# Attention over pairs of heads: transposes of scaled probabilities, one instruction per pair, queues shifted by a pair

## The chip, the cores and the metric

One core of one Trainium2 chip. The time is that of one execution of the program on the device, in microseconds (us). Engines: TensorE (PE; its weight loads are listed as PEld), VectorE (DVE), ScalarE (ACT), GpSimd (POOL) and SyncE (SP, which issues the DMAs). L1972 is line 1972 of the kernel before; in the kernel after, the same code stands up to 8 lines earlier, and the transposes are recorded at the helper `turn` (L1572 there).

## The reference, cut to what matters

A two-layer backbone over 256 context and 256 latent tokens of width 1024 in float32. Each layer has a gated FFN, a mixer and a second gated FFN. The mixer of the second layer is neighbourhood attention: 16 heads of 64, latent queries on a grid of 4 rows by 64 columns, softmax over the local window and all context keys together.

```python
s_loc = jnp.where(col_valid[:, :, None, :], s_loc + bias, NEG_INF)
s_ctx = jnp.einsum('bjqhd,bkhd->bhjqk', qb, k_c).astype(jnp.float32)
s = jnp.concatenate([s_loc.reshape(B, H, n_cb, NA_QBLOCK_W, n_loc), s_ctx], axis=-1)
p = jax.nn.softmax(s, axis=-1).astype(v_g.dtype)
...
o = (jnp.einsum('bhjqil,bijlhd->bjqhd', p_loc, v_blk)
     + jnp.einsum('bhjqk,bkhd->bjqhd', p_ctx, v_c))
```

## The kernel before

The program is written by hand: each engine has one list of instructions, and semaphores tie them together. The large projections run as three passes each of values split into a high and a low part (`three`, L1582 to L1586). ScalarE makes the high parts, VectorE the low ones, SyncE fetches weight tiles two ahead.

Both mixers have a function `mixer1` or `mixer0` on every engine. The attention is the last part of `mixer1`, after the keys, queries and values are projected. It has 32 units, one for each head and half of the 256 queries. Two heads that lie in the two 64-partition halves of one tile make a pair with the same half of the queries, so there are 16 pairs; `pair_of(j)` gives the tile (j // 2), the half s, and `at`, the first of the pair's two places among four (0 or 2). Everything is sized 128 queries by 512 keys per unit. For unit u of pair j:

- TensorE `scores_of` (L1960): one fp32 matmul with 64 rows, the two heads side by side in the two halves of the array, into one PSUM bank each. Pairs take turns between `ps_all[0:2]` and banks 2 and 3. From pair 2 on it waits for the exponentials of pair j - 2.
- VectorE `maxima`: adds the bias to the 256 local keys in PSUM (L1464), takes the negated maximum over 512 keys (L1467). One instruction per unit.
- ScalarE `exps` (L889): exponential from PSUM to SBUF, and the row's sum through the accumulator. The results lie in `prob`, which uses the buffers named scaled and normed.
- VectorE `diagonals`: the reciprocal of the sum (L1476), then the identity times it, a diagonal of 128x128 (L1480).
- TensorE `turn_probs` (L1972): four matmuls of a 128x128 block of the probabilities against the diagonal, which turn and normalise it in one step, into `ps[1]`, one bank per unit. `ps[1]` has no second copy, so the turn waits for the copy of the pair before.
- ScalarE `copy_turned` (L899): from PSUM to `prob_t`, 512 elements per unit.
- TensorE `outputs_of` (L1985): eight matmuls with 64 output rows, two heads side by side, for the pair before.
- every second pair, ScalarE `high` (L904) and VectorE `low` (L1486) split a finished tile for the projection na_out.

The order of each queue is set by these loops: TensorE `turn_probs(j)`, `scores_of(j + 2)`, `outputs_of(j - 1)`; ScalarE `copy_turned(j)`, `exps(j + 2)`; VectorE `maxima(j + 2)`, `diagonals(j + 2)`. After the last outputs, TensorE goes on with na_out, whose last step waits for the last split.

`turn` (L1578) is a helper used elsewhere in the program: `pe.transpose` against the identity. Lines 1729 (fp32 matmuls of 128x128), 962 (an operation of 1024 elements), 1086 and 1384 (VectorE in the norms and in the first mixer), 1308 and 1309 (VectorE, 512 elements) and 877 (a ScalarE copy of 1024 elements from PSUM) belong to other stages and serve the prediction as prices.

## Time and profile before

| | |
|---|---|
| median of 3 runs | 1903.8 us (1902.56 to 1903.91) |
| profiled execution | 1899.26 us, span 1897.5 us, mean granted clock 0.976 |
| PE busy | 1813.9 us (96% of the span) |
| DVE busy | 1207.3 us (64%) |
| ACT busy | 748.8 us (39%) |
| attention, first scores to last outputs | 1588.6 to 1656.9 us from the span's start |

The span runs from the first to the last instruction of the profiled execution; its own time lies 1.8 us above. Busy times are shares of the whole span and mix stages with different limits. Times of rows are microseconds from the span's start. A fp32 matmul is two records on PE, a transpose one. Where two matmuls run side by side in two halves of the array, each has its own records.

### The profile page before, as it was taken

How to read it: one execution, taken by the hardware profiler on the slowest of the kernel's cores; microseconds unless marked ns; L12 is line 12 of the kernel's file. 1: busy time of each engine (PE TensorE's matmuls, PEld its weight loads, DVE VectorE, ACT ScalarE, POOL GpSimd, SP SyncE). 2: the span in 40 equal slices, each digit the busy share in tenths (PEclk: the TensorE clock that was granted, in tenths of full speed). 3: DMA queues.
4: the chain of work that ended last, by engine and by line, in shares of the span. 5: the costliest groups of instructions: out<-in, count | busy, mean ns of one | idle time of the engine just before them, and what ended most of it. 6: DMA issues, size and time to landing. Idle time of an engine off the chain costs nothing.

```text
span 1897.5 us, 25311 instructions
## 1 busy us (share of the span) xinstructions
PE 1813.9 (96%) x9680; PEld 1531.0 (81%) x9680; DVE 1207.3 (64%) x1908; ACT 748.8 (39%) x1067; POOL 62.7 (3%) x40
## 2 busy tenths in 40 slices
PE   6899999999989798999999999999999999989998
PEld 2788888877788587888888878888887797789998
DVE  4777677778999744876677367766333435655554
ACT  2522122347888734222222352222223434654343
POOL 0000000020000010000000200000002000010001
PEclk8999999999999998999999999999999999989999
DMA  7454555331110122544553344453323341034553
GB/s 300 156 188 163 181 190 209 113 115 67 47 55 34 45 89 101 190 185 150 196 210 117 114 155 177 150 190 147 111 69 108 122 167 45 1 127 169 178 183 120
DMA packets 39860, 257.74 MB, mean 136 GB/s; under 512 B 4688, under 2 KB 5840, under 8 KB 14832
## 3 DMA queue, kind: packets, MB, share of 16 engines
q1 hardware_dynamic: 39792, 256.86, 37.3%
q8 instruction: 40, 0.66, 0.1%
q14 instruction: 28, 0.23, 0.0%
HBM read 255.79 MB, written 1.05 MB: 135 GB/s over the span
## 4 chain that ended last, share of the span: by engine, by line
PE 84%; DVE 9%; ACT 4%; issue 2%; DMA 1%; SPq 0%; DVEq 0%; ACTq 0%
PE ps_all L1582 26%; PE ps_all L1586 26%; PE ps_all L1583 25%; DVE w_lo L950 2%; PE ps_all L1972 2%; PE bank L1630 1%; DMA start_scale<-in_w_scale 1%; ACT w_hi L535 1%; PE bank L1985 1%; DVE sq_acc L1300 1%; PE bank L2008 1%; PE ps_all L1960 0%; DVE normed L1309 0%; DVE wb L1264 0%; DVE scaled L1291 0%
## 5 line engine op out<-in xcount | busy, mean ns | idle before, releaser
L1582 PE MATMUL ps_all<-a_hi,w_lo 128*128 128x512 f32 (+1 forms) x1800 | 663.2, 368 | 21.4 <-ACT a_hi L645 14.2
L1586 PE MATMUL ps_all<-a_lo,w_hi 128*128 128x512 f32 (+1 forms) x1800 | 657.9, 366 | 0.2 <-DVE a_lo L1089 0.2
L1583 PE MATMUL ps_all<-a_hi,w_hi 128*128 128x512 f32 (+1 forms) x1800 | 657.4, 365 | 0.0
L950 DVE TENSOR_TENSOR w_lo<-w_raw,w_hi 128x2048 fp32r<-128x2048 f32 (+3 forms) x184 | 376.5, 2046 | 162.7 <-ACT w_hi L535 161.6
L535 ACT ACTIVATE w_hi<-w_raw 128x2048 fp32r<-128x2048 f32 (+3 forms) x183 | 313.5, 1713 | 332.0 <-PE ps_all L1586 324.1
L1582 PEld LDWEIGHTS ps_all<-a_hi,w_lo 128*128 128x128 f32 x1800 | 345.4, 192 | 79.4 <-issue 16.5
L1586 PEld LDWEIGHTS ps_all<-a_lo,w_hi 128*128 128x128 f32 x1800 | 345.1, 192 | 56.6 <-DVE a_lo L1089 4.1
L1583 PEld LDWEIGHTS ps_all<-a_hi,w_hi 128*128 128x128 f32 x1800 | 345.8, 192 | 51.8 <-issue 0.2
L962 DVE SCALAR_TENSOR_TENSOR mod_junk<-mod_raw,cond 128x1024 bf16<-128x1024 f32 x256 | 302.7, 1220 | 5.0 <-ACT cond L563 2.7
L1582 PE MATMUL ps_all<-g_hi,w_lo 128*128 128x512 f32 (+1 forms) x704 | 257.8, 366 | 1.2 <-DVE w_lo L950 1.2
L1586 PE MATMUL ps_all<-g_lo,w_hi 128*128 128x512 f32 (+1 forms) x704 | 256.3, 364 | 0.0
L1583 PE MATMUL ps_all<-g_hi,w_hi 128*128 128x512 f32 (+1 forms) x704 | 254.3, 361 | 0.0
L546 ACT ACTIVATE sil<-ps_all 128x512 f32<-128x512 f32 (+1 forms) x88 | 47.8, 543 | 483.6 <-PE ps_all L1586 483.5
L988 DVE TENSOR_TENSOR gated<-sil,ps_all 128x512 f32<-128x512 f32 (+1 forms) x88 | 54.6, 621 | 193.8 <-ACT sil L546 193.8
L1027 DVE SCALAR_TENSOR_TENSOR h<-ps_all,gate,h 128x256 f32 (+1 forms) x136 | 59.9, 480 | 168.8 <-PE ps_all L1586 168.1
L1586 PEld LDWEIGHTS ps_all<-g_lo,w_hi 128*128 128x128 f32 x704 | 132.2, 188 | 23.2
L1583 PEld LDWEIGHTS ps_all<-g_hi,w_hi 128*128 128x128 f32 x704 | 132.2, 188 | 22.0
L1582 PEld LDWEIGHTS ps_all<-g_hi,w_lo 128*128 128x128 f32 x704 | 132.5, 188 | 21.6 <-DVE w_lo L950 1.9
L549 ACT ACTIVATE g_hi<-gated 128x512 f32 (+3 forms) x88 | 51.0, 579 | 69.2 <-DVE gated L988 69.2
L995 DVE TENSOR_TENSOR g_lo<-gated,g_hi 128x512 f32 (+3 forms) x88 | 54.8, 623 | 27.7 <-ACT g_hi L549 27.7
L1547 POOL TENSOR_TENSOR sq_acc<-sq 128x512 f32<-128x512 f32 (+1 forms) x6 | 11.9, 1977 | 1732.0 <-ACT sq L582 1732.0
L645 ACT ACTIVATE a_hi<-scaled,modv,gain 128x256 fp32r<-128x256 f32 x88 | 48.4, 592 | 22.4 <-DVE scaled L1077 22.4
(234 smaller groups left out, 1493.3 us busy)
## 6 DMA issues: line engine op xcount, KB each, us to landing
w_raw<-in_tiles SPq DMA_DIRECT2D x118, 1024.0 KB, 4.7
mod_raw<-in_w_mod SPq DMA_DIRECT2D x64, 1024.0 KB, 4.8
w_raw<-in_tiles SPq DMA_DIRECT2D x32, 768.0 KB, 4.1
w_raw<-in_tiles SPq DMA_DIRECT2D x32, 640.0 KB, 3.8
start_raw<-in_w_mod SPq DMA_DIRECT2D x4, 1024.0 KB, 16.2
start_scale<-in_w_scale SPq DMA_DIRECT2D x4, 1024.0 KB, 20.4
bias<-in_na_bias SPq DMA_DIRECT2D x2, 1536.0 KB, 8.9
cond<-in_cond SPq DMA_DIRECT2D x2, 1024.0 KB, 6.1
```

The source lines that it names most:

```text
L535: nc.scalar.activation(w_hi[:, slot, 0:size], w_raw[:, slot, 0:size], ACT.Copy).then_inc(hi_ready, 1)
L546: nc.scalar.activation(sil[:, slot, t0:T], ps[slot][:, 0, t0:T], ACT.Silu).then_inc(sil_ready, 1)
L549: nc.scalar.activation(g, gated[:, slot, t0:T], ACT.Copy).then_inc(g_hi_ready, 1)
L645: ins = nc.scalar.activation(a_hi[:, k, b:e], scaled[:, k % 2, b:e], ACT.Identity, bias=modv[:, col(k_norm, 0) + k, half:half + 1], scale= ...
L950: nc.vector.tensor_tensor(w_lo[:, slot, 0:size], w_raw[:, slot, 0:size], w_hi[:, slot, 0:size].bitcast(F32), ALU.subtract).then_inc(lo_rea ...
L962: nc.vector.scalar_tensor_tensor(junk[:, v], raw[:, c], 1.0, cond[:, v], ALU.mult, ALU.mult, accum_out=mod_acc[:, acc, c, v:v + 1]).then_i ...
L988: nc.vector.tensor_tensor(gated[:, slot, t0:T], sil[:, slot, t0:T], ps[slot][:, 1, t0:T], ALU.mult).then_inc(ps_free[slot], 1)
L995: nc.vector.tensor_tensor(lo, gated[:, slot, t0:T], hi.bitcast(F32), ALU.subtract).then_inc(g_split, 1)
L1027: ins = nc.vector.scalar_tensor_tensor(h[:, bass.ds(at + m, 1), b:e].rearrange("p a t -> p (a t)"), ps[slot][:, m, b:e], gated_by[:, half, ...
L1582: pe.matmul(dst, w[1], x[0], start=start, stop=False)
L1583: pe.matmul(dst, w[0], x[0], start=False, stop=False)
L1586: return pe.matmul(dst, w[0], x[1], start=False, stop=stop_)
```

## The change

- `diag` and its semaphore go. VectorE's `scale_probs` multiplies the probabilities in place by the reciprocal of their sum, 128x512 per unit, and `turn_probs` transposes them against the identity with `turn`.
- The four banks of PSUM become one tensor, so that bias, maximum, reciprocal, and the copy of the turned probabilities are one instruction per pair.
- The queues are shifted: the scores of pair j + 3 are issued behind the outputs of pair j - 1, three pairs of scores stand ahead of the first turn, `scale_probs(j + 1)` follows `maxima(j + 2)`, and `exps(j + 1)` stands ahead of `copy_turned(j)`.

```diff
@@ -228,7 +228,8 @@
 
         ps_all = ctx.enter_context(nc.psum_tensor("ps_all", [P, 4, 512], F32))
         ps = [ps_all[:, 2 * n:2 * n + 2] for n in range(2)]
-        bank = [ctx.enter_context(nc.psum_tensor(f"bank{n}", [P, 512], F32)) for n in range(4)]
+        banks = ctx.enter_context(nc.psum_tensor("banks", [P, 4, 512], F32))
+        bank = [banks[:, n] for n in range(4)]
         ps_mod, ps_sum = bank[2], bank[3]
         glu_to = [[ps[0][:, 0, :], ps[0][:, 1, :]], [bank[2][:], bank[0][:]]]
 
@@ -293,7 +294,6 @@
             k_t = sbuf("k_t", [P, KT, T], F32, na)
             v_tok = sbuf("v_tok", [P, 4, D], F32, na)
             prob_t = sbuf("prob_t", [P, 4, T], F32, na)
-            diag = sbuf("diag", [P, 4, P], F32, na)
             negmax = sbuf("negmax", [P, UNITS], F32, na)
             rowsum = sbuf("rowsum", [P, UNITS], F32, na)
             recip = sbuf("recip", [P, UNITS], F32, na)
@@ -328,7 +328,7 @@
             "loads", "gam_in", "qk", "swapped", "rope", "gam", "exp1", "slope", "least", "cross", "exp2", "mask", "s", "p", "o",
             "osq", "kept", "gated", "sum", "std", "rstd", "spread", "mixed", "cast", "mix", "y_split", "ymix")}
         na_sem = {n: sem("na_" + n) for n in (
-            "bias", "masked", "s", "added", "max", "exp", "recip", "diag", "turned", "copied", "o",
+            "bias", "masked", "s", "added", "max", "exp", "recip", "scaled", "turned", "copied", "o",
             "hi", "mix")}
         out_stored = sem("out_stored")
 
@@ -401,7 +401,7 @@
                 return None
             return first + per * (it - begin) + slot if begin else first + per * it + slot
 
-        score_bank = [ps_all[:, 0, :], ps_all[:, 1, :], bank[2][:, :], bank[3][:, :]]
+        score_bank = [ps_all[:, 0:2, :], banks[:, 2:4, :]]
 
         PAIRS = UNITS // 2
 
@@ -881,12 +881,12 @@
                 def exps(j):
 
                     _, _, at = pair_of(j)
+                    act.wait_ge(N["max"], j + 1)
+                    if j >= 2:
+                        act.wait_ge(N["turned"], 2 * j - 2)
                     for n in range(2):
                         u = 2 * j + n
-                        act.wait_ge(N["max"], u + 1)
-                        if j >= 2:
-                            act.wait_ge(N["turned"], u - 3)
-                        nc.scalar.activation(prob[at + n], score_bank[at + n], ACT.Exp, bias=negmax[:, u:u + 1],
+                        nc.scalar.activation(prob[at + n], score_bank[j % 2][:, n], ACT.Exp, bias=negmax[:, u:u + 1],
                                              accum_out=rowsum[:, u:u + 1]).then_inc(N["exp"], 1)
 
                 def copy_turned(j):
@@ -894,9 +894,8 @@
                     _, _, at = pair_of(j)
                     if j >= 2:
                         act.wait_ge(N["o"], 2 * j - 2)
-                    for n in range(2):
-                        act.wait_ge(N["turned"], 2 * j + n + 1)
-                        nc.scalar.activation(prob_t[:, at + n, :], ps[1][:, n, :], ACT.Copy).then_inc(N["copied"], 1)
+                    act.wait_ge(N["turned"], 2 * j + 2)
+                    nc.scalar.activation(prob_t[:, at:at + 2, :], ps[1][:, :, :], ACT.Copy).then_inc(N["copied"], 1)
 
                 def high(tile):
 
@@ -907,11 +906,10 @@
                         ACT.Copy).then_inc(N["hi"], 1)
 
                 exps(0)
-                exps(1)
                 for j in range(PAIRS):
+                    if j + 1 < PAIRS:
+                        exps(j + 1)
                     copy_turned(j)
-                    if j + 2 < PAIRS:
-                        exps(j + 2)
                     if j >= 2 and j % 2 == 0:
                         high(j // 2 - 1)
                 high(PAIRS // 2 - 1)
@@ -1457,28 +1455,23 @@
                 def maxima(j):
 
                     tile, s, at = pair_of(j)
+                    dve.wait_ge(N["s"], 2 * j + 2)
+                    local = score_bank[j % 2][:, :, NCTX:T]
+                    nc.vector.tensor_tensor(local, local, bias[:, 2 * tile:2 * tile + 2, 2 - 2 * s:6 - 2 * s, :].rearrange("p h r c -> p h (r c)"),
+                                            ALU.add).then_inc(N["added"], 1)
+                    dve.wait_ge(N["added"], j + 1)
+                    nc.vector.tensor_reduce(negmax[:, 2 * j:2 * j + 2], score_bank[j % 2], AX.X, ALU.max,
+                                            negate=True).then_inc(N["max"], 1)
+
+                def scale_probs(j):
+
+                    _, _, at = pair_of(j)
+                    dve.wait_ge(N["exp"], 2 * j + 2)
+                    nc.vector.reciprocal(recip[:, 2 * j:2 * j + 2], rowsum[:, 2 * j:2 * j + 2]).then_inc(N["recip"], 1)
+                    dve.wait_ge(N["recip"], j + 1)
                     for n in range(2):
-                        u = 2 * j + n
-                        dve.wait_ge(N["s"], u + 1)
-                        local = score_bank[at + n][:, NCTX:T]
-                        nc.vector.tensor_tensor(local, local, bias[:, 2 * tile + n, 2 - 2 * s:6 - 2 * s, :].rearrange("p r c -> p (r c)"),
-                                                ALU.add).then_inc(N["added"], 1)
-                        dve.wait_ge(N["added"], u + 1)
-                        nc.vector.tensor_reduce(negmax[:, u:u + 1], score_bank[at + n], AX.X, ALU.max,
-                                                negate=True).then_inc(N["max"], 1)
-
-                def diagonals(j):
-
-                    _, _, at = pair_of(j)
-                    for n in range(2):
-                        u = 2 * j + n
-                        dve.wait_ge(N["exp"], u + 1)
-                        nc.vector.reciprocal(recip[:, u:u + 1], rowsum[:, u:u + 1]).then_inc(N["recip"], 1)
-                        dve.wait_ge(N["recip"], u + 1)
-                        if j >= 2:
-                            dve.wait_ge(N["turned"], u - 3)
-                        nc.vector.tensor_scalar(diag[:, at + n, :], const[:, C_IDENT:C_IDENT + P], recip[:, u:u + 1], None,
-                                                ALU.mult).then_inc(N["diag"], 1)
+                        nc.vector.tensor_scalar(prob[at + n], prob[at + n], recip[:, 2 * j + n:2 * j + n + 1], None,
+                                                ALU.mult).then_inc(N["scaled"], 1)
 
                 def low(tile):
 
@@ -1490,13 +1483,14 @@
                         ALU.subtract).then_inc(N["mix"], 1)
 
                 dve.wait_ge(N["masked"], 4)
-                for j in range(2):
-                    maxima(j)
-                    diagonals(j)
+                maxima(0)
+                maxima(1)
+                scale_probs(0)
                 for j in range(PAIRS):
                     if j + 2 < PAIRS:
                         maxima(j + 2)
-                        diagonals(j + 2)
+                    if j + 1 < PAIRS:
+                        scale_probs(j + 1)
                     if j >= 2 and j % 2 == 0:
                         low(j // 2 - 1)
                 low(PAIRS // 2 - 1)
@@ -1957,26 +1951,24 @@
                         pe.wait_ge(N["exp"], 2 * j - 2)
                     for n in range(2):
                         rows = slice(64 * n, 64 * n + 64)
-                        pe.matmul(score_bank[at + n], q_t[rows, tile, s * P:(s + 1) * P], k_t[rows, tile, :],
+                        pe.matmul(score_bank[j % 2][:, n], q_t[rows, tile, s * P:(s + 1) * P], k_t[rows, tile, :],
                                   start=True, stop=True).then_inc(N["s"], 1)
 
                 def turn_probs(j):
 
                     _, _, at = pair_of(j)
+                    if j:
+                        pe.wait_ge(N["copied"], j)
                     for n in range(2):
-                        u = 2 * j + n
-                        pe.wait_ge(N["diag"], u + 1)
-                        if j:
-                            pe.wait_ge(N["copied"], u - 1)
+                        pe.wait_ge(N["scaled"], 2 * j + n + 1)
                         for t in range(4):
-                            mm = pe.matmul(ps[1][:, n, t * P:(t + 1) * P], prob[at + n][:, t * P:(t + 1) * P], diag[:, at + n, :],
-                                           start=True, stop=True)
+                            mm = turn(ps[1][:, n, t * P:(t + 1) * P], prob[at + n][:, t * P:(t + 1) * P])
                         mm.then_inc(N["turned"], 1)
 
                 def outputs_of(j):
 
                     tile, s, at = pair_of(j)
-                    pe.wait_ge(N["copied"], 2 * j + 2)
+                    pe.wait_ge(N["copied"], j + 1)
                     if s == 0 and tile >= 2:
                         pe.wait_ge(N["mix"], tile - 1)
                     for t in range(4):
@@ -1989,12 +1981,13 @@
 
                 scores_of(0)
                 scores_of(1)
+                scores_of(2)
                 for j in range(PAIRS):
                     turn_probs(j)
-                    if j + 2 < PAIRS:
-                        scores_of(j + 2)
                     if j:
                         outputs_of(j - 1)
+                    if j + 3 < PAIRS:
+                        scores_of(j + 3)
                 outputs_of(PAIRS - 1)
                 for j in range(4):
                     pair_tile("na_out", j, 8, 0, lambda k: pe.wait_ge(N["mix"], k + 1) if j == 0 else None, NCTX)
```

How the queues read, at the three places that matter. TensorE at the start of the attention, before: the second half of scores 1 (`bank`), then the turn of pair 0 (`diag`, and the probabilities in `scaled`), then scores 2.

```order
L1960 MATMUL bank<-k_t,q_t 128x512 x2
L1972 MATMUL ps_all<-diag,scaled 128x128 [waits na_diag]
L1972 MATMUL ps_all<-diag,scaled 128x128 x3
L1972 MATMUL ps_all<-diag,scaled 128x128 [waits na_diag]
L1972 MATMUL ps_all<-diag,scaled 128x128 x3
L1960 MATMUL ps_all<-k_t,q_t 128x512 [waits na_exp]
```

The same place in the change:

```order
L1954 MATMUL banks<-k_t,q_t 128x512 x2
L1954 MATMUL ps_all<-k_t,q_t 128x512 [waits na_exp]
L1954 MATMUL ps_all<-k_t,q_t 128x512
L1572 MATMUL ps_all<-const,scaled 128x128 [waits na_scaled]
L1572 MATMUL ps_all<-const,scaled 128x128 x3
```

Scores 2, which wait for the exponentials of pair 0, have moved ahead of the turn of pair 0; the turn waits for the scaling instead of the diagonal.

TensorE in the running pattern, before: scores 3, outputs 0, the first half of turn 2.

```order
L1960 MATMUL bank<-k_t,q_t 128x512 [waits na_exp]
L1960 MATMUL bank<-k_t,q_t 128x512
L1985 MATMUL bank<-prob_t,v_tok 64x128 [waits na_copied]
L1985 MATMUL bank<-prob_t,v_tok 64x128 x7
L1972 MATMUL ps_all<-diag,scaled 128x128 [waits na_copied,na_diag]
L1972 MATMUL ps_all<-diag,scaled 128x128 x3
```

In the change: outputs 0, scores 4, the first half of turn 2.

```order
L1977 MATMUL banks<-prob_t,v_tok 64x128 [waits na_copied]
L1977 MATMUL banks<-prob_t,v_tok 64x128 x7
L1954 MATMUL ps_all<-k_t,q_t 128x512 [waits na_exp]
L1954 MATMUL ps_all<-k_t,q_t 128x512
L1572 MATMUL ps_all<-const,scaled 128x128 [waits na_scaled,na_copied]
L1572 MATMUL ps_all<-const,scaled 128x128 x3
```

Outputs and scores have changed places, and the scores are a pair further ahead.

VectorE in the running pattern, before: maxima of one pair, then the first of the two diagonals of the same pair.

```order
L1464 TENSOR_TENSOR ps_all<-ps_all,bias 128x256 [waits na_s]
L1467 TENSOR_REDUCE negmax<-ps_all 128x1 [waits na_added]
L1464 TENSOR_TENSOR ps_all<-ps_all,bias 128x256 [waits na_s]
L1467 TENSOR_REDUCE negmax<-ps_all 128x1 [waits na_added]
L1476 RECIPROCAL recip<-rowsum 128x1 [waits na_exp]
L1480 TENSOR_SCALAR diag<-const,recip 128x128 [waits na_turned,na_recip]
```

In the change: the maxima of pair 2, then the scaling of pair 1 (its probabilities lie in `normed`).

```order
L1460 TENSOR_TENSOR ps_all<-ps_all,bias 128x2x256 [waits na_s]
L1463 TENSOR_REDUCE negmax<-ps_all 128x2 [waits na_added]
L1470 RECIPROCAL recip<-rowsum 128x2 [waits na_exp]
L1473 TENSOR_SCALAR normed<-normed,recip 128x512 [waits na_recip]
L1473 TENSOR_SCALAR normed<-normed,recip 128x512
```

Eight instructions a pair have become five, the last two four times as wide as a diagonal, and the reciprocal now belongs to the pair before the one whose maxima were just taken.

## Rows read from the trace of the kernel before

**Rows 1.** The page's chain that ended last, shares of the whole span.

```profile
PE 84%; DVE 9%; ACT 4%; issue 2%; DMA 1%; SPq 0%; DVEq 0%; ACTq 0%
```

**Rows 2.** The chain in 1586 to 1662: start, us, engine, tile, line.

```profile
1621.56 1.98 PE ps_all L1972 x16
1623.54 1.06 PE bank L1960 x4
1624.60 1.02 PE bank L1985 x16
...
1655.00 1.90 PE bank L1985 x32
```

**Rows 3.** Windows: length, busy us (count) of each engine, PE clock, DMA share, GB/s.

```profile
528.00:532.00 4.00, 2.52 (x31) 2.24 (x29) 3.85 (x11) 3.95 (x7) 0.00 (x0) 1.00 0.00 0
...
1592.00:1595.50 3.50, 3.04 (x16) 2.87 (x16) 2.91 (x10) 1.56 (x4) 0.00 (x0) 0.67 0.00 0
1595.50:1599.00 3.50, 3.50 (x21) 2.37 (x20) 2.50 (x8) 2.35 (x6) 0.00 (x0) 0.85 0.02 5
...
1600.00:1648.00 48.00, 48.00 (x432) 36.03 (x432) 37.03 (x101) 31.96 (x80) 0.00 (x0) 1.00 0.01 1
```

**Rows 4.** Waits in 1588 to 1658: total us, times, longest.

```profile
ACT scaled L889 <- DVE negmax L1467: 11.7, 16, 1.3
```

**Rows 5.** PE groups by form (busy us, mean ns), and eight transposes from the timeline.

```profile
L1578 PE MATMUL bank<-const,wb 128*128 128x128 f32 x64 | 9.6, 275 | 4.1 <-DVE scaled L1292 4.1
L1729 PE MATMUL bank<-us,sq 128*128 128x128 f32 x128 | 16.8, 276 | 0.7 <-ACT sq L749 0.7
...
461.93 1.03 PE L1578 MATMUL bank<-const,wb 128*128 128x128 f32 x8
```

**Rows 6.** DVE groups by form over the whole span: busy us, mean ns.

```profile
L1467 DVE TENSOR_REDUCE negmax<-ps_all 128x1 f32<-128x512 f32 x16 | 11.1, 691 | 0.6
L962 DVE SCALAR_TENSOR_TENSOR mod_junk<-mod_raw,cond 128x1024 bf16<-128x1024 f32 x256 | 302.7, 1220 | 5.0 <-ACT cond L563 2.7 <-DMA mod_raw<-in_w_mod 1.9 <-DVE gate L1038 0.4
L1476 DVE RECIPROCAL recip<-rowsum 128x1 f32<-128x1 f32 x32 | 5.1, 158 | 7.2 <-ACT normed L889 3.6 <-ACT scaled L889 3.6
L1480 DVE TENSOR_SCALAR diag<-const,recip 128x128 f32<-128x128 f32 x32 | 9.2, 287 | 1.4 <-DVE recip L1476 0.3
L1086 DVE TENSOR_SCALAR normed<-scaled,gain,modv 128x256 f32<-128x256 f32 x40 | 16.5, 412 | 1.1
L1384 DVE CAST a_hi<-cond 128x512 fp32r<-128x512 f32 x4 | 1.7, 427 | 0.1
L1486 DVE TENSOR_TENSOR a_lo<-bank,a_hi 128x256 fp32r<-128x256 f32 x8 | 3.4, 419 | 4.4 <-ACT a_hi L904 4.4
```

**Rows 7.** DVE timeline: start, us, line; the starts of neighbours give the spacing.

```profile
501.40 0.69 DVE L1308 TENSOR_TENSOR normed<-sq_acc,tcos 128x512 f32<-128x512 f32 x1
502.01 0.69 DVE L1309 TENSOR_TENSOR normed<-sq_acc,tsin 128x512 f32<-128x512 f32 x1
...
1589.79 0.43 DVE L1464 TENSOR_TENSOR ps_all<-ps_all,bias 128x256 f32<-128x256 f32 x1 [7.07 <-PE ps_all L1960]
...
1621.04 0.69 DVE L1467 TENSOR_REDUCE negmax<-ps_all 128x1 f32<-128x512 f32 x1
...
1621.64 0.42 DVE L1464 TENSOR_TENSOR ps_all<-ps_all,bias 128x256 f32<-128x256 f32 x1
```

**Rows 8.** ACT groups by form over the whole span: busy us, mean ns.

```profile
L889 ACT ACTIVATE scaled<-ps_all,negmax 128x512 f32<-128x512 f32 x16 | 11.0, 687 | 11.7 <-DVE negmax L1467 11.7
L889 ACT ACTIVATION_READ_ACCUMULATOR scaled<-ps_all,negmax 128x1 f32 x16 | 3.1, 193 | 0.0
L877 ACT ACTIVATE v_tok<-ps_all 128x1024 f32<-128x1024 f32 x4 | 4.1, 1023 | 35.1 <-PE ps_all L1586 35.1
```

**Rows 9.** The chain in 656 to 673, PE alone: one matmul of 512 at each clock.

```profile
657.32 0.23 PE bank L1583
...
672.44 0.43 PE ps_all L1583
```

## The prediction

> **What bounds the kernel now.** I read the page's chain first, to see which engine sets the end, then the chain inside the attention stage, then its windows, the waits, and last the rows of single operations. The chain of the whole run is 84% TensorE [rows 1], and the change touches only the attention over 16 pairs of heads (from 1588.6 us, the first score matmul, to 1656.9 us, where the first tile of na_out begins). Inside it the chain is a repeating triple, all on TensorE [rows 2]: the eight turning matmuls of a pair 1.98 us, its score matmuls 1.06, its output matmuls 1.02. The period is 1.98 + 1.06 + 1.02 = 4.06 us a pair. The window from 1600 to 1648 says the same: TensorE busy 48.00 of 48.00 us, VectorE 37.03, ScalarE 31.96, clock 1.00 [rows 3]. The waits of the other engines (ScalarE 11.7 us for the maxima of even pairs, [rows 4]) cost nothing here. So the stage gets shorter by whatever leaves TensorE, until VectorE is full.
>
> **The change part by part, against the profiled execution (1899.26 us, span 1897.5).**
>
> *TensorE.* Gone are 8 fp32 matmuls a pair against a diagonal; in come 8 transposes against the identity. The trace has the same instruction elsewhere: line 1578 transposes 128x128 fp32 blocks, 64 calls in 64 records, while line 1729 uses two records for each of its plain fp32 matmuls (64 calls, 128 records) [rows 5]. Eight transposes ran in 1.03 us, the last taking 0.27, so one starts every (1.03 - 0.27) / 7 = 0.108 us; a plain matmul of this shape takes 1.98 / 8 = 0.248 [rows 2, 5]. A pair turns in 8 x 0.108 = 0.87 us, and TensorE needs 0.87 + 1.06 + 1.02 = 2.95 us a pair.
>
> *VectorE.* Before, per pair: two adds of 256 elements, two maxima of 512, two reciprocals, two diagonals of 128. After: one add of 512, one maximum over 1024, one reciprocal, two in-place scalings of 128x512.
> - Add: 512 elements take 0.69 us (the 512-element maximum reads the same bank [rows 6]), and the dependent maximum starts 0.03 after its end: 0.72.
> - Maximum: no row has a reduction of 1024. The line 962 operation of 1024 elements takes 1.22 [rows 6], and the next instruction starts before the end of the last one (0.60 after a start where one takes 0.69 [rows 7]), so 1.14.
> - Reciprocal: 0.158, with its hand-over 0.19.
> - Scalings: the diagonal, the same operation with a per-partition factor, took 287 ns for 128 elements, and line 1086, also with per-partition factors, 412 for 256 [rows 6]: 0.98 ns an element, so 0.66 to 0.69 for 512. Operations of 512 start 0.61 apart [rows 7]. Two: 1.21.
> - The low parts of the result (0.42 [rows 6], so 0.35 with the overlap) come every other pair: 0.18.
>
> Sum: 0.72 + 1.14 + 0.19 + 1.21 + 0.18 = 3.44 us a pair, against TensorE's 2.95. **VectorE becomes the bound**, and the gain is 4.06 - 3.44 = 0.62 us a pair, not the 1.11 that leave TensorE. The ends of this price: were the scaling done at the rate of the cast of 512 elements (427 ns [rows 6]), two would cost 0.69 and the sum 2.92; I take 3.44, because both rows with a per-partition factor lie on the one-element line. The maximum of 1024 could lie anywhere between two of 512 (1.38) and 1.14; the upper end adds 0.24 x 16 = 3.8 us, and I keep it for the range.
>
> The Trainium skill ("VectorE: DVE Perf Modes", section "The perf-mode tier table") gives tensor_scalar on fp32 in SBUF two elements a cycle and tensor_tensor one. This trace does not agree for a per-partition factor, which costs 0.98 ns an element, the step from 287 to 412 ns. By the page the pair would cost VectorE 2.92 us, and TensorE would stay the bound.
>
> *ScalarE.* Two exponentials (0.69 each, plus two reads of the sum, at most 0.19 each), one copy of 1024 (1.02) [rows 8], and every other pair a cast of 256 elements, which I count as half an exponential at most: under 3.13 us. It hides under 3.44.
>
> *Order.* VectorE now scales pair j+1 after the maxima of pair j+2, so the 1.5 us of exponentials lie under 1.86 us of maxima and the reciprocal no longer waits. The scores of pair j+3 must be ready when the scaling of pair j+1 ends. From the end of scaling j: half a turn 0.44, outputs 1.02, scores 1.06, hand-overs 0.2, together 2.7 us, while VectorE has 3.26 us of work. It fits, with half a microsecond of room. It does not fit at half clock.
>
> *Beginning.* The turn of pair 0 now stands behind scores 2, which wait for both exponentials of pair 0. VectorE starts at 1589.8 [rows 7]; add and maximum 1.9 us, the two exponentials about 1.5 (two of 0.69, the first read of a sum partly under the next), so TensorE has nothing from 1590.6 to 1593.2. Before, it was idle there too, for a shorter time, and the granted clock fell to its lower level: 0.67 from 1592 to 1595.5 and 0.85 to 1599, together some 1.7 us of clock lost, that is 3.4 us at 1.2 GHz [rows 3]. I expect the same fall. Matmul rates at that level are 1.87 times slower (0.43 us a matmul for 0.23, line 1583 at the two levels [rows 9]), so scores 2 end at 1595.3, and VectorE, done with scaling 0 at 1594.9, waits about 0.5.
>
> *End.* Scaling 15 waits some 0.2 for the last exponentials. After it TensorE still has the turn (1.05, with a wait for the copy of pair 14), outputs 14 (1.02), 0.25 of waiting for the last copy, which is now one of 1.02 for both heads, and outputs 15 (1.02): 3.3 us.
>
> **Sum.** 1589.8 + 16 x 3.26 + 6 x 0.35 (low parts ahead of scaling 15) + 0.5 + 0.2 = 1644.8; plus 3.3 = 1648.1, where before outputs 15 end at 1655.0 + 1.9 = 1656.9 [rows 2]. The stage is **8.8 us** shorter. Behind it nothing moves: the split of the second na_out tile, the norm and the last FFN hang on the end of outputs 15 as before. The profiled execution would take 1890.5 us. It lies 4.5 under the median of the runs, 1903.8, so for the median I say 1903.8 - 8.8 = **1895.0 us**. What a measurement here can tell from no change is 0.2%, 3.8 us.
>
> **The rivals.**
> - *Scaling at two elements a cycle.* TensorE is then the bound with 2.95. After 1593.2 it has 14 scores, 16 turns and 16 outputs, 45.0 us, plus 1.6 for the low clock and 2 of waits at both ends: 1641.8, gain 15, **1888.8 us**. For it speaks the cast of 427 ns, against it the two rows with factors [rows 6].
> - *The clock comes back late.* Transposes are a quarter of TensorE's work now, and if they do not count for the clock as matmuls do, the low level lasts for two or three stretches instead of one. One or two more of 3.4 us cost about 1 to 2.7 us together: **1896 to 1898**.
> - *The clock stays low through the stage: the side of slower.* At 1.2 GHz a pair costs TensorE 2.95 x 1.87 = 5.5 us, so 45.0 x 1.87 = 84.2 us after 1593.2 end at 1677.4, 20.5 later than before: **1924 us**. The place is the beginning, where the clock falls anyway. Each microsecond at the low level costs 1 - 3.44 / 5.5 = 0.37 us against the forecast, so from about 24 us of it (four to five pairs) the gain is gone. Against it: in the S5 stage TensorE was busy for only 2.52 of 4.00 us, none of it transposes, and was granted 1.00 throughout [rows 3], and here it would be busy for 2.95 of 3.44, 2.08 of it in matmuls. And at the low level TensorE, being the bound, has no idle time, which is what preceded the fall.
> - *The transposes cost what the matmuls cost.* Then the period stays 4.06 and only the later beginning shows, about 1 us: **1905 us**. The records of line 1578 speak against it.
>
> The second and third rivals rest on what the rows cannot decide, whether transposes count. The Trainium skill ("TensorE: Matmul & The Clock Gate", section "Part 4: PE-mode transpose") says that the full clock does not engage for transposes, which do not count as busy in the same way. No run here shows a stretch of transposes long enough to agree or disagree.
>
> **Chances.** Forecast 0.72; fast scaling 0.10; late clock 0.07; low clock throughout 0.05; costly transposes 0.06. The range goes from the fast scaling, 1888.8, to the late clock and the dear maximum, 1895.0 + 3.8 = 1898.8, rounded to 1899; outside lie the last two rivals and a rest. Its likeliest case alone would be 1892 to 1899. Faster by over 0.2% are the first three, less 0.02 for small things added up: 0.87. The costly transposes and that rest make 0.08, the low clock 0.05.
>
> **What would show it.** In the profile after: transposes one record each, starting 0.11 us apart; scalings of 0.66 to 0.69 us; VectorE busy through 1600 to 1640 with TensorE at about 86%; starts of the adds 3.26 and 3.61 us apart by turns; the clock back at 1.00 by 1600; na_out beginning near 1648. Scalings of 0.43, a clock of 0.50 after 1600, or adds 4 us apart would each prove another case.

## The result and the profile after

Over five runs each the kernel after took 1889.46 us and the kernel before 1903.61: ratio 0.9929, 95% interval 0.9917 to 0.9940. The medians lie 14.2 us apart, and the interval allows 11 to 16 us. Repeated later (e9) the ratio was 0.9934 (0.9920 to 0.9947), with medians 12.3 us apart. The forecast was 1895.0 us, 8.8 us shorter. The direction and the place were right; the gain was about one and a half times the forecast.

| kernel | attention, first scores to na_out | per pair | what differs from the kernel after |
|---|---|---|---|
| before | 68.2 us | 4.06 us | |
| after | 54.4 | 3.11 | |
| e1 | 70.0 | 4.06 | plain matmuls for transposes |
| e2 | 77.9 | 4.63 | queues in the old order |
| e3 | 59.8 | 3.48 | one instruction per unit |
| e4 | 55.3 | 3.11 | other factors in the scalings |
| e5 | 54.4 | 3.11 | one scaling a pair |
| e6 | 59.7 | 3.42 | three scalings a pair |
| e7, e10 | 54.2, 54.1 | 3.11 | shorter ends |
| e8 | 56.6 | 3.16 | one wait per turn |
| e9 | 55.3 | 3.11 | nothing |

The attention is read from the timeline of each profile, from the first score matmul to the first matmul of na_out; the time per pair is a sixth of the distance from the outputs of pair 3 to those of pair 9. The stage is 68.2 - 54.4 = 13.8 us shorter, which is the gain within its interval. The spans of the two profiled executions differ by only 1897.5 - 1887.6 = 9.9 us, mainly because in the one of after the stage began at 1593.4 instead of 1588.6; what lies behind the stage took 240.7 us before and 239.9 after. Kernels that are the same up to there began it anywhere from 1588.6 to 1594.8, so lengths of the stage are compared below, and times only where they come from several runs. Each length is that of one execution. Kernels with the same bound gave the same length to a tenth: 54.4 in after and e5, 55.3 in e4 and e9. These two values differ by a fall of the granted clock from 1.00 to 0.50 a few microseconds into the stage, which some executions had and some had not. The execution of before had it, so like with like the stage is 68.2 - 55.3 = 12.9 us shorter (e9).

The chain inside the attention after, the view of [rows 2]: start, us, engine, tile, line. L1572 are the transposes, L1977 the outputs, L1954 the scores.

```profile
1614.50 1.02 PE ps_all L1572 x8
1615.53 1.02 PE banks L1977 x16
1616.55 1.06 PE ps_all L1954 x4
...
1642.21 1.08 PE ps_all L1572 x8
...
1643.37 1.04 ACT prob_t L898
1644.45 1.11 PE ps_all L1572 x8
...
1645.64 1.03 ACT prob_t L898
1646.72 1.09 PE banks L1977 x16
```

The repeating triple is still all TensorE: the turn has gone from 1.98 to 1.02 us, the other two are as they were, 3.11 a pair. At the end, copy and turn of the last two pairs follow one another.

The windows after, as in [rows 3]: the beginning, then the running pattern.

```profile
1593.40:1598.00 4.60, 1.96 (x8) 0.71 (x8) 3.32 (x4) 2.52 (x5) 0.00 (x0) 1.00 0.00 0
1598.00:1601.40 3.40, 3.21 (x16) 1.46 (x16) 3.30 (x7) 2.60 (x7) 0.00 (x0) 1.00 0.00 0
...
1604.00:1636.00 32.00, 32.00 (x288) 20.40 (x284) 30.84 (x59) 26.73 (x59) 0.00 (x0) 1.00 0.01 2
```

TensorE is busy for 32.00 of 32 us and VectorE for 30.84: TensorE is still the bound, with VectorE close behind; two engines this full need a test of which one leads, and e5 is that test. I had TensorE at 86%. And the clock did not fall at the beginning of this execution.

VectorE's groups by form after, which answer to [rows 6]: busy us, mean ns.

```profile
L1463 DVE TENSOR_REDUCE negmax<-ps_all 128x2 f32<-128x1024 f32 x8 | 9.8, 1224 | 0.3
L1473 DVE TENSOR_SCALAR scaled<-scaled,recip 128x512 f32<-128x512 f32 x16 | 7.1, 484 | 0.3
L1460 DVE TENSOR_TENSOR ps_all<-ps_all,bias 128x512 f32<-128x512 f32 x8 | 5.6, 699 | 7.6 <-PE ps_all L1954 7.1
L1470 DVE RECIPROCAL recip<-rowsum 128x2 f32<-128x2 f32 x16 | 2.5, 155 | 0.5 <-ACT normed L889 0.5
```

Add, maximum and reciprocal cost what the sum had for them (0.69, 1.22 and 0.16 us). The scaling did not: 484 ns, for a forecast of 0.66 to 0.69. VectorE's timeline shows what that makes of a pair:

```profile
1617.68 0.70 DVE L1460 TENSOR_TENSOR ps_all<-ps_all,bias 128x512 f32<-128x512 f32 x1
1618.42 1.22 DVE L1463 TENSOR_REDUCE negmax<-ps_all 128x2 f32<-128x1024 f32 x1
1619.56 0.15 DVE L1470 RECIPROCAL recip<-rowsum 128x2 f32<-128x2 f32 x1
1619.75 0.88 DVE L1473 TENSOR_SCALAR normed<-normed,recip 128x512 f32<-128x512 f32 x2
1620.55 0.42 DVE L1479 TENSOR_TENSOR a_lo<-banks,a_hi 128x256 fp32r<-128x256 f32 x1
1620.88 0.69 DVE L1460 TENSOR_TENSOR banks<-banks,bias 128x512 f32<-128x512 f32 x1
```

From start to start: 0.74 + 1.14 + 0.19 + 0.80 = 2.87, and 0.33 for the low part every other pair, so 3.04 a pair where the sum had 3.44.

### The profile page after: what moved, and what is told of

Read it like the earlier page. It is cut to its first block, busy times and chain, and to the rows that moved or that the text cites. A ratio compares the mean times of both kernels' runs of the same rounds, so it can differ in the third digit from the quotient of the medians.

```text
span 1887.6 us, 24934 instructions
## 1 busy us (share of the span) xinstructions
PE 1803.5 (96%) x9552; PEld 1518.0 (80%) x9552; DVE 1205.7 (64%) x1860; ACT 747.6 (40%) x1051; POOL 62.7 (3%) x40
## 4 chain that ended last, share of the span: by engine, by line
PE 84%; DVE 9%; ACT 4%; issue 2%; DMA 1%; SPq 0%; DVEq 0%; ACTq 0%
PE ps_all L1576 26%; PE ps_all L1580 26%; PE ps_all L1577 26%; DVE w_lo L948 2%; PE banks L1624 1%; DMA start_scale<-in_w_scale 1%; DVE sq_acc L1298 1%; ACT w_hi L535 1%; PE banks L2001 1%; PE ps_all L1572 1%; PE banks L1977 1%; PE banks L1791 1%; DVE normed L1307 0%; DVE wb L1262 0%; DVE scaled L1289 0%
## 5 line engine op out<-in xcount | busy, mean ns | idle before, releaser
L1576 PE MATMUL ps_all<-a_hi,w_lo 128*128 128x512 f32 (+1 forms) x1800 | 662.4, 368 | 21.5 <-ACT a_hi L645 14.2
L960 DVE SCALAR_TENSOR_TENSOR mod_junk<-mod_raw,cond 128x1024 bf16<-128x1024 f32 x256 | 302.8, 1221 | 4.8 <-ACT cond L563 2.7
L986 DVE TENSOR_TENSOR gated<-sil,ps_all 128x512 f32<-128x512 f32 (+1 forms) x88 | 54.6, 621 | 193.9 <-ACT sil L546 193.9
```

The source lines that it names most:

```text
L960: nc.vector.scalar_tensor_tensor(junk[:, v], raw[:, c], 1.0, cond[:, v], ALU.mult, ALU.mult, accum_out=mod_acc[:, acc, c, v:v + 1]).then_i ...
L986: nc.vector.tensor_tensor(gated[:, slot, t0:T], sil[:, slot, t0:T], ps[slot][:, 1, t0:T], ALU.mult).then_inc(ps_free[slot], 1)
L1576: pe.matmul(dst, w[1], x[0], start=start, stop=False)
```

## The experiments

**e1: is it the transposes?** The same queues and merged instructions, but plain matmuls.

```diff
-                            mm = turn(ps[1][:, n, t * P:(t + 1) * P], prob[at + n][:, t * P:(t + 1) * P])
+                            mm = pe.matmul(ps[1][:, n, t * P:(t + 1) * P], prob[at + n][:, t * P:(t + 1) * P], const[:, C_IDENT:C_IDENT + P],
+                                           start=True, stop=True)
```

> The kernel after, with each transpose written as an ordinary fp32 matmul against the identity; merging, scaling and the shifted queues stay. Theory (TensorE sets the pace, and the shorter turn is the source of the gain): eight turning matmuls cost 1.98 us again for 1.02, a pair 1.98 + 1.06 + 1.02 = 4.06 us, the attention 67 to 69 us for 54.5 in the kernel after, the time that of the kernel before within 2 us. Rival (the shift and the merging bring the gain, the transposes little): attention under 60 us and a time still 8 us or more under the kernel before. VectorE should show about 0.75 busy in the running pattern, no more.

Measured: 0.9999 of the kernel before (0.9989 to 1.0008), attention 70.0 us. The timeline of TensorE in e1 (L1965 is the turn), start and us:

```profile
1613.15 1.13 PE L1954 MATMUL ps_all<-k_t,q_t 64*128 64x512 f32 x4
1614.21 2.05 PE L1965 MATMUL ps_all<-const,scaled 128*128 128x128 f32 x16
1616.19 1.09 PE L1978 MATMUL banks<-prob_t,v_tok 128*64 128x128 f32 x16
1617.22 1.13 PE L1954 MATMUL banks<-k_t,q_t 64*128 64x512 f32 x4
```

Sixteen records and 1.98 us to the next group, 4.06 a pair as before. Without the transposes nothing is gained: merging and shifting alone free engines that nobody waits for. The stage is even 1.8 us longer than before, and a microsecond over the range I expected. With the same time per pair, the difference lies in the beginning and the end.

**e2: does the order matter?** The kernel after, with the three engines' loops as they were.

```diff
                 scores_of(0)
                 scores_of(1)
-                scores_of(2)
                 for j in range(PAIRS):
                     turn_probs(j)
+                    if j + 2 < PAIRS:
+                        scores_of(j + 2)
                     if j:
                         outputs_of(j - 1)
-                    if j + 3 < PAIRS:
-                        scores_of(j + 3)
...
-                maxima(0)
-                maxima(1)
-                scale_probs(0)
+                for j in range(2):
+                    maxima(j)
+                    scale_probs(j)
                 for j in range(PAIRS):
                     if j + 2 < PAIRS:
                         maxima(j + 2)
-                    if j + 1 < PAIRS:
-                        scale_probs(j + 1)
+                        scale_probs(j + 2)
```

> The kernel after with the queue orders of the kernel before (scores two ahead in front of the outputs, exponentials two ahead behind the copy, scaling directly behind the maxima of its own pair). Theory (the shift hides the exponentials from VectorE): VectorE now waits for both exponentials of a pair, about 1.5 us, in every pair: add 0.74, maximum 1.22, exponentials 1.5, reciprocal 0.19, scalings 0.80, half a low part 0.17, together 4.6 us a pair and an attention of 75 to 80 us, that is slower than the kernel before by 7 to 12 us. Rival (the order is indifferent once TensorE has less to do): attention 54 to 57 us.

Measured: 1.0045 of the kernel before (1.0030 to 1.0061), attention 77.9 us. VectorE in e2:

```profile
1615.04 1.22 DVE L1464 TENSOR_REDUCE negmax<-banks 128x2 f32<-128x1024 f32 x1
1617.78 0.17 DVE L1471 RECIPROCAL recip<-rowsum 128x2 f32<-128x2 f32 x1 [1.51 <-ACT normed L889]
1617.98 0.89 DVE L1474 TENSOR_SCALAR normed<-normed,recip 128x512 f32<-128x512 f32 x2
```

In each of the 16 pairs the reciprocal stands behind 1.51 us of waiting for the exponentials. This is the wait that the shift by a pair takes away. With transposes and merging but without the shift, the kernel is slower than before. The edit changes the order on three engines at once, so it does not say which of the three orders matters most.

**e3: what is merging worth?** One instruction per unit again; for the maxima the edit is below, and the copy, the reciprocal and the waits on their semaphores follow it.

```diff
-                    dve.wait_ge(N["s"], 2 * j + 2)
-                    local = score_bank[j % 2][:, :, NCTX:T]
...
-                    nc.vector.tensor_reduce(negmax[:, 2 * j:2 * j + 2], score_bank[j % 2], AX.X, ALU.max,
-                                            negate=True).then_inc(N["max"], 1)
+                    for n in range(2):
+                        u = 2 * j + n
+                        dve.wait_ge(N["s"], u + 1)
+                        local = score_bank[j % 2][:, n, NCTX:T]
...
+                        nc.vector.tensor_reduce(negmax[:, u:u + 1], score_bank[j % 2][:, n], AX.X, ALU.max,
+                                                negate=True).then_inc(N["max"], 1)
```

> The kernel after with one instruction per unit instead of per pair for bias, maximum, reciprocal and copy; transposes and shifted queues stay. Theory (VectorE has almost no room, so its fixed costs count): two adds 0.46, two maxima 0.61, two reciprocals 0.19, two scalings 0.40, half a low part 0.17 make 3.49 us a pair, above TensorE's 3.10; attention 59 to 61 us, 5 to 6 us longer than in the kernel after. Rival (TensorE alone is the bound, merging is worth nothing): attention 54 to 55 us and 3.10 us a pair.

Measured: 0.9952 of the kernel before (0.9935 to 0.9968), attention 59.8 us, 3.48 a pair. Here VectorE is the bound: its instructions follow one another without a gap, from start to start 2 x (0.46 + 0.61 + 0.19 + 0.40) and 0.17 for half a low part, together 3.49. What it has over the 3.04 of the kernel after are the fixed costs of one add, one maximum and one reciprocal. Merging is worth 0.37 us a pair, which is all there is between VectorE's 3.48 and TensorE's 3.11.

**e4: what does a scaling cost?** The first unit is multiplied by 0.5, the second multiplied by one factor and added to another, so the probabilities are not normalised by their own sums.

```diff
-                    for n in range(2):
-                        nc.vector.tensor_scalar(prob[at + n], prob[at + n], recip[:, 2 * j + n:2 * j + n + 1], None,
-                                                ALU.mult).then_inc(N["scaled"], 1)
+                    nc.vector.tensor_scalar(prob[at], prob[at], 0.5, None, ALU.mult).then_inc(N["scaled"], 1)
+                    nc.vector.tensor_scalar(prob[at + 1], prob[at + 1], recip[:, 2 * j + 1:2 * j + 2], recip[:, 2 * j:2 * j + 1],
+                                            ALU.mult, ALU.add).then_inc(N["scaled"], 1)
```

> The kernel after, where the first unit of a pair is multiplied by an immediate 0.5 and the second multiplied by one per-partition factor and added to another; so the probabilities are not normalised by their own sums. It measures what a scaling of 128x512 fp32 costs. Theory now (two elements a cycle always, and about 60 ns for each per-partition factor: 160 + 267 ns with none, 217 + 267 with one as the 484 in the kernel after, 280 + 267 with two): 0.43 us for the first, 0.55 for the second. Rival, as forecast (one element a cycle with a per-partition factor): 0.69 or more for the second. Attention 54 to 55 us in either case of the first kind.

Measured, the groups of the two lines in e4:

```profile
L1473 DVE TENSOR_SCALAR scaled<-scaled,recip 128x512 f32<-128x512 f32 x8 | 4.3, 541 | 0.0
L1472 DVE TENSOR_SCALAR scaled<-scaled 128x512 f32<-128x512 f32 x8 | 3.4, 427 | 0.3
```

The attention took 55.3 us, with a fall of the clock at its beginning, of which more below. With no per-partition factor 427 ns, with one 484 (the kernel after), with two 541: each factor adds 57 ns. What an element costs follows from rows with the same number of factors. With one, 287 ns for the 128 elements of line 1480 and 484 for 512 make (484 - 287) / 384 = 0.51 ns an element. With two, 412 for the 256 of line 1086 and 541 for 512 make 0.50. So a factor adds a fixed amount and leaves the rate alone. A tensor_tensor costs twice as much an element: line 950 of the kernel before took 1221 ns for 1024 elements and 2289 for 2048, that is 1.04.

The form with two factors also has a second arithmetic operation, which could be what costs. Two groups of the kernel before speak against it. Line 1143 has two operations with two immediates, line 1115 one of each:

```profile
L1115 DVE TENSOR_SCALAR stat<-stat 128x32 f32<-128x32 f32 x17 | 3.1, 180 | 0.5
L1143 DVE TENSOR_SCALAR stat<-stat 128x32 f32<-128x32 f32 x1 | 0.2, 181 | 0.0
```

The second operation costs nothing there. These rows with immediates also give the rate: (427 - 180) / 480 = 0.51.

**e5: which engine sets 3.11?** The scaling of the second unit is left out, so half of the probabilities are not normalised.

```diff
-                    for n in range(2):
-                        nc.vector.tensor_scalar(prob[at + n], prob[at + n], recip[:, 2 * j + n:2 * j + n + 1], None,
-                                                ALU.mult).then_inc(N["scaled"], 1)
+                    nc.vector.tensor_scalar(prob[at], prob[at], recip[:, 2 * j:2 * j + 1], None,
+                                            ALU.mult).then_inc(N["scaled"], 2)
```

> The kernel after without the scaling of the second unit of each pair, which is then not normalised. Theory (TensorE sets 3.10 us a pair, VectorE at about 3.05 only follows): VectorE drops to 2.65 us a pair and the period stays 3.10; attention 53.9 to 54.6 us (54.4 in the kernel after, or 1 more where the clock falls at its beginning). Rival (VectorE sets the pace, as forecast): the period falls to 2.95 or less and the attention to 52 us.

Measured: attention 54.4 us, 3.11 a pair, as in the kernel after to a tenth of a microsecond. The running pattern:

```profile
1604.00:1636.00 32.00, 32.00 (x294) 20.87 (x294) 27.04 (x47) 25.88 (x58) 0.00 (x0) 1.00 0.01 2
```

VectorE's busy time fell from 30.84 to 27.04 us, and neither the time per pair nor the stage moved. TensorE sets the pace.

**e6: was the rest of the forecast right?** A third scaling a pair, into a buffer that is idle, gives VectorE the load of the forecast.

```diff
                                                 ALU.mult).then_inc(N["scaled"], 1)
+                        if n == 0:
+                            nc.vector.tensor_scalar(sq[:, 0, :], sq[:, 1, :], recip[:, 2 * j:2 * j + 1], None, ALU.mult)
```

> The kernel after with one more scaling of 128x512 a pair on VectorE, whose result nobody reads. It puts VectorE at 3.05 + 0.40 = 3.45 us a pair, the load that the forecast gave it. Theory (the forecast had only the price of the scalings wrong): period 3.43 to 3.46 us, attention 59 to 60 us, which is 8.5 to 9 us shorter than before, as forecast. Rival (something else in the forecast was wrong as well, a wait in the shifted order): attention over 61 or under 57 us.

Measured: attention 59.7 us, 3.42 a pair. The running pattern:

```profile
1604.00:1636.00 32.00, 31.14 (x262) 18.78 (x260) 31.37 (x62) 24.22 (x54) 0.00 (x0) 1.00 0.00 1
```

The busy times are too close to tell the bound: TensorE's 31.14 takes in most of the waiting inside a turn, whose records now span 1.24 to 1.36 us instead of 1.09, because the extra scaling stands between the two that a turn waits for. The spacing of the outputs tells it:

```profile
1619.08 1.09 PE L1979 MATMUL banks<-prob_t,v_tok 128*64 128x128 f32 x16
1622.33 1.09 PE L1979 MATMUL banks<-prob_t,v_tok 128*64 128x128 f32 x16
1625.91 1.09 PE L1979 MATMUL banks<-prob_t,v_tok 128*64 128x128 f32 x16
```

They come 3.25 and 3.58 us apart by turns, and 0.33 is VectorE's low part, which falls into every other pair. VectorE has taken over as the bound, and the stage is 68.2 - 59.7 = 8.5 us shorter than before, where the forecast said 8.8. The pieces agree as well: from the first scores to the end of the last scaling 56.1 us for a forecast of 56.2, and 3.6 behind it for 3.3. With the load that I had worked out, the kernel does what I had worked out.

**e7 and e10: a shorter beginning and end.** Bias and maximum of pair 0 per unit; the copy of pair 14 per unit; the copy of the last unit on VectorE; two low parts later.

```diff
+                    for n in range(2 if j == PAIRS - 2 else 1):
+                        act.wait_ge(N["turned"], 2 * j + n + 1)
+                        nc.scalar.activation(prob_t[:, at + n, :], ps[1][:, n, :], ACT.Copy).then_inc(N["copied"], 1)
...
+                dve.wait_ge(N["turned"], 2 * PAIRS)
+                nc.vector.tensor_copy(prob_t[:, 3, :], ps[1][:, 1, :]).then_inc(N["copied"], 1)
```

> The kernel after with shorter ends: pair 0 has its bias and maximum per unit, the copy of pair 14 is made per unit so that turn 15 starts after half of it, the copy of the last unit goes to VectorE beside ScalarE's, and two low parts move behind the last scalings. Theory (after the pattern of 3.10 us has ended, and before it has begun, single chains set the time, some 4 us in all): attention 52.6 to 53.4 us, 1 to 1.8 shorter than the 54.4 of the kernel after. Rival (the ends are hidden under the queue of TensorE): 54.2 to 54.6 us.

The profile of e7 gave 54.2 us, outside my range of 52.6 to 53.4 and at the edge of the rival's 54.2 to 54.6. But it can't be compared with the 54.4: in this execution the clock fell at the beginning, and in that of the kernel after it had not. So both were run again together.

> The kernel after, unchanged, on the same chip and in the same rounds as the next one. Attention 54.4 us in the profile, or about 55.3 where the granted clock falls 4.6 us after the first scores. Time against the kernel before: 13 to 14 us shorter.

> The kernel with the shorter ends again, timed. Its profile gave 54.2 us with the fall of the clock, where another kernel with the same body and the fall had 55.3, so about 1.1 us less. Theory: 1 to 1.5 us under the kernel after in the time, which is under the 0.2% that a measurement can tell, and 53.1 to 54.3 us of attention, by whether the clock falls. Rival (the difference of one profile was chance): attention 54.4 or 55.3 us as in the kernel after.

Measured, both with the fall: 55.3 us for the kernel after (e9), 54.1 for the shorter ends (e10). The times were 0.9934 (0.9920 to 0.9947) and 0.9924 (0.9911 to 0.9938) of the kernel before, medians 1889.32 and 1887.79. The 1.2 us are there in the stage; the intervals of the times overlap, as they must for a difference under 0.1%, so a gain in time is not shown. The chain at the end of e7 (L1595 turns, L2002 outputs) shows where 0.7 of them are (from the start of outputs 12 to na_out it is 6.8 us, in the kernel after 7.4). The rest is at the beginning: the first outputs start 10.2 us after the first scores in e7 and 10.6 in e9.

```profile
1640.73 1.07 PE ps_all L1595 x8
1641.80 1.02 PE banks L2002 x16
1642.82 1.02 PE ps_all L1595 x8
1643.85 1.90 PE banks L2002 x32
```

The last turns and outputs follow one another without a copy between them.

**e8: the 0.15 us that a turn costs beyond its transposes.**

```diff
-                    for n in range(2):
-                        pe.wait_ge(N["scaled"], 2 * j + n + 1)
+                    pe.wait_ge(N["scaled"], 2 * j + 2)
+                    for n in range(2):
```

> The kernel after with one wait for both scalings ahead of the eight transposes instead of one ahead of each four. A turn took 1.02 us where eight transposes at 0.108 are 0.87. Theory (the rest is the hand-over from one group of matmuls to the next, which a wait inside the turn does not change): turn 1.00 to 1.02, period 3.10. Rival (the wait between the two units costs it): turn 0.90 to 0.96 and period about 3.0.

Measured: a turn of 0.99 us, but 3.16 a pair and an attention of 56.6 us. Neither the theory nor the rival had a longer period. The timeline of TensorE in e8:

```profile
1612.46 1.06 PE L1572 MATMUL ps_all<-const,scaled 128*128 128x128 f32 x8
1613.45 1.09 PE L1977 MATMUL banks<-prob_t,v_tok 128*64 128x128 f32 x16
1614.48 1.13 PE L1954 MATMUL banks<-k_t,q_t 64*128 64x512 f32 x4
1615.59 1.06 PE L1572 MATMUL ps_all<-const,normed 128*128 128x128 f32 x8
```

The wait inside a turn costs some 0.03 us; the rest of the 0.15 stays. It was not tried further whether it belongs to the change from one group to the next. But the stage is longer than the kernel after's (1.3 us more than e9, which like it had the fall), and from the start of the scores to the next turn it is 1.11 us here for a group that takes 1.06. In every other pair VectorE's add now waits 0.18 us for the scores, and the turn waits for VectorE's scaling. My reading, which no further run tested, is that the first four transposes can no longer run under the second scaling, and that VectorE, at 3.04 of 3.11 us, is so near the bound that this delay of some 0.4 us shows.

## Why the prediction was right and wrong

The measured 1889.46 us lies inside the range of 1888.8 to 1899, but 0.7 us above its lower end. That end was the time of the fast scaling, a rival with a chance of 0.10; the forecast's own case alone was given 1892 to 1899 and missed. The range held because it reached down to that rival; the mechanism of the forecast, VectorE as the bound, did not come.

- *What bounds before, and that transposes take a record each and start 0.108 us apart*: right, or nearly. A turn of eight is 8 records; over a whole turn of the kernel after the spacing is (1.09 - 0.27) / 7 = 0.117. A turn takes 1.02 us, not 0.87: I took the spacing inside a run of eight and left out what a group costs around its transposes, though the 1.98 us of before had it too. That makes 3.11 a pair where I had 2.95.
- *VectorE's scalings*: the step that failed. "Two: 1.21" should have been 0.80. I drew a line through the 287 ns of line 1480 and the 412 ns of line 1086 and read its slope, 0.98 ns an element, as the rate. But the first has one per-partition factor and the second two, and each costs 57 ns (e4), so the line joined two different operations. The rate is 0.51. The cast of 512 elements in 427 ns had the right rate; I gave it a chance of 0.10 because both rows with factors seemed to speak against it. The Trainium skill ("VectorE: DVE Perf Modes", section "The perf-mode tier table") gives tensor_scalar on fp32 in SBUF twice the rate of tensor_tensor. I had set this aside, and it holds here for all three forms: 0.50 to 0.51 ns an element against 1.04; the 57 ns stand beside it.
- *"VectorE becomes the bound"* failed with it: at 3.04 against 3.11 it does not (e5). e6 puts VectorE back to 3.42 and finds 8.5 us of gain for 8.8, with the last scaling at 56.1 for 56.2, so order, hand-overs and beginning of the sum held, and its end within 0.3 us.
- The rival of fast scaling was the one that came, in a weaker form: it gave 2.92 for VectorE, 2.95 for TensorE and 1888.8 us. The measured 3.11 for TensorE took back 16 x 0.16 = 2.6 us of its gain of 15, and what it had allowed for the low clock, 1.6, was lost in some executions only, and then as 0.9. That its 1888.8 lies so near the 1889.46 is therefore in part luck.
- *The order*: the adds come 3.20 and 3.02 us apart by turns, not 3.61 and 3.26; right that the shift hides 1.5 us of exponentials; taking it away costs more than the whole gain (e2). I had priced the fit at "half a microsecond of room", for VectorE's 3.26 of work; at 3.11 a pair, e8 shows how little of it is left.
- *Beginning*: "I expect the same fall" was right for some executions only. The clock fell 4.5 to 4.7 us after the first scores in those of before, e1, e2, e4 and e6 to e10, and not in those of after, e3 and e5. The kernel after with and without it: 55.3 and 54.4, one execution each, so the fall costs 0.9 us where I had 0.5.
- *Late and low clock*: neither came in the kernel after. The windows of e9 where the clock fell:

```profile
1595.40:1598.80 3.40, 3.33 (x10) 1.83 (x11) 2.50 (x6) 1.47 (x5) 0.00 (x0) 0.51 0.00 0
1598.80:1602.20 3.40, 3.34 (x32) 2.18 (x30) 3.33 (x6) 2.94 (x6) 0.00 (x0) 0.99 0.00 0
```

In the first, scores 2 (2.08 us) and the transposes of turn 0 (1.69 from 1597.55 on) fill TensorE at 0.51, and then 0.99 is granted. The transposes, a third of TensorE's work in the kernel after, did not keep the clock down. By the Trainium skill ("TensorE: Matmul & The Clock Gate", section "Part 4: PE-mode transpose") they would not count as busy in the same way; if so, it made no difference here, and no run was all transposes.

## What to carry to other kernels

Before a line is drawn through two rows, the operands must be of the same kind: a second per-partition factor costs as much as 110 elements (57 ns at 0.51 ns each). A gain found on the bounding engine is worth no more than the distance to the next one, so the next engine's instructions deserve the same care as the ones that go. Transposes, merging and the shifted order need one another: without the first the gain was 0, without the third the kernel was slower than before, without the second 8.4 of 13.8 us were left (neither execution had the fall of the clock). None of the three was run alone.

## What was not expected of the hardware

- A per-partition factor of a VectorE fp32 tensor_scalar costs 57 ns fixed, and two cost 114 (427, 484 and 541 ns at 512 elements), while the elements go at 0.50 to 0.51 ns.
- The clock's fall at the beginning of the stage depends on the execution, not on the kernel: the same program had it in one profile and not in another.
- How long the low level lasted differed. In e2 it stayed for 10.2 us, with TensorE waiting in the first two of these windows; in the kernel after (e9) for 3.4, with TensorE filled. Why was not tried further. The windows of e2:

```profile
1595.00:1598.40 3.40, 2.53 (x10) 2.08 (x12) 2.88 (x5) 0.38 (x3) 0.00 (x0) 0.50 0.00 0
1598.40:1601.80 3.40, 2.72 (x10) 1.27 (x7) 2.14 (x5) 2.08 (x5) 0.00 (x0) 0.50 0.00 0
1601.80:1605.20 3.40, 3.40 (x16) 1.56 (x16) 1.85 (x5) 2.36 (x5) 0.00 (x0) 0.50 0.02 5
```
